# Two-layer model on one core: norm split between projection and scores, delta rule's gate behind the first naming, both key sides named together

## What is computed

```python
h2 = _rmsnorm(x, norm2[l])                    # x * rsqrt(mean(x*x) + EPS) * g
q = (xf @ w_pq).reshape(n_tok, P_HEADS, 2, P_DHALF)
s = jnp.einsum('thpd,phkd->thpk', q, sub_keys)
top_s, top_i = lax.top_k(s, P_TOPK)           # 16 of 128 keys on either side
cand_s = (top_s[:, :, 0, :, None] + top_s[:, :, 1, None, :]).reshape(...)
cand_i = (top_i[:, :, 0, :, None] * N_KEYS + top_i[:, :, 1, None, :]).reshape(...)
best_s, pos = lax.top_k(cand_s, P_TOPK)       # 16 of 256 pairs
idx = jnp.take_along_axis(cand_i, pos, axis=-1)
gate = jax.nn.softmax(best_s)
u = expert_u[it]
h = jax.nn.gelu(jnp.einsum('td,tkd->tk', xt, u), approximate=False)
v = expert_v[it]
y = jnp.einsum('tk,tkd->td', gt * h, v)       # 128 experts of every token
```

## Time and profile before

| | us |
|---|---|
| median of 3 runs | 1746.54 |
| lowest, highest | 1746.27, 1746.67 |
| span of the profiled execution | 1748.2 |
| TensorE, VectorE, ScalarE, GpSimd busy | 1545.4, 979.4, 440.9, 318.8 |
| gathers on GpSimd (L828), main and panels | 251.3 and 59.4 |

### The profile page before, as it was taken

One profiled execution on the slowest core, in us unless ns is written; L12 is line 12 of the kernel. 1 busy time (PEld: TensorE's weight loads), 2 busy tenths in 40 slices (PEclk: granted clock), 3 DMA queues, 4 the chain that ended last, 5 costly groups with the idle time before them and its releaser, 6 DMA issues.

```text
span 1748.2 us, 20696 instructions
## 1 busy us (share of the span) xinstructions
PE 1545.4 (88%) x8336; PEld 1016.7 (58%) x8336; DVE 979.4 (56%) x1882; ACT 440.9 (25%) x1004; POOL 318.8 (18%) x271
## 2 busy tenths in 40 slices
PE   8999999998988879878577676679999999999998
PEld 7867555557454534445233222249995486599953
DVE  3444443216877863579986656644755415356654
ACT  1143452103355631233243222221000024210001
POOL 0000000002135543343464454500000000000000
PEclk9999999999989989999789887899999999999999
DMA  5364222267999999999999999993453523354432
GB/s 226 145 223 163 98 97 97 109 247 319 425 385 406 424 419 389 421 422 415 422 420 421 422 422 421 422 382 145 151 188 145 201 94 127 130 196 163 175 144 96
DMA packets 55343, 468.32 MB, mean 268 GB/s; under 512 B 6736, under 2 KB 8144, under 8 KB 10704
## 3 DMA queue, kind: packets, MB, share of 16 engines
q0 software_dynamic: 36864, 268.45, 37.1%
q1 hardware_dynamic: 18384, 198.55, 29.9%
HBM read 465.93 MB, written 1.05 MB: 267 GB/s over the span
## 4 chain that ended last, share of the span: by engine, by line
PE 65%; DMA 17%; DVE 11%; issue 3%; ACT 2%; POOL 2%; SPq 0%; DVEq 0%; POOLq 0%; ACTq 0%
DMA main<-in_expert_uv,main 14%; PE ps L2401 14%; PE ps L2347 7%; PE ps L438 7%; PE ps L918 7%; PE ps L394 6%; PE ps L2558 6%; PE ps L2326 3%; DVE main L846 3%; PE ps L220 3%; DMA panels<-in_wall 2%; PE ps L2322 2%; PE ps L2633 2%; PE ps L434 2%; POOL main L828 1%
## 5 line engine op out<-in xcount | busy, mean ns | idle before, releaser
L918 PE MATMUL ps<-main 128*128 128x512 f32 x660 | 337.4, 660 | 120.8 <-ACT main L893 120.8
L828 POOL DMA_INDIRECT main<-in_expert_uv,main x208 | 251.3, 1208 | 381.9 <-PE ps L918 185.6
L846 DVE SCALAR_TENSOR_TENSOR main<-main 128x1024 f32<-128x1024 f32 x208 | 250.0, 1223 | 114.9 <-DMA main<-in_expert_uv,main 114.0
L918 PEld LDWEIGHTS ps<-main 128*128 128x128 f32 x660 | 132.6, 210 | 304.2 <-ACT main L893 161.0
L2347 PE MATMUL ps<-xT,panels 128*128 128x256 f32 x576 | 128.7, 386 | 1.8 <-DMA panels<-in_wall 1.8
L2347 PEld LDWEIGHTS ps<-xT,panels 128*128 128x128 f32 x576 | 111.1, 194 | 18.2 <-DMA panels<-in_wall 2.1
L881 ACT ACTIVATE main<-main 128x2 f32<-128x2 f32 x128 | 26.0, 203 | 365.6 <-DVE main L846 297.7
L394 PE MATMUL ps<-panels,xT 128*128 128x512 f32 x256 | 113.5, 597 | 0.0
L2401 PE MATMUL ps<-main 128*128 128x128 f32 x912 | 104.9, 275 | 0.0
L2401 PEld LDWEIGHTS ps<-main 128*128 128x128 f32 x912 | 103.4, 192 | 0.0
L918 PE MATMUL ps<-panels,main 128*128 128x512 f32 x152 | 76.3, 647 | 22.8 <-ACT main L893 22.8
(11 more groups left out here) (342 smaller groups left out, 2170.4 us busy)
## 6 DMA issues: line engine op xcount, KB each, us to landing
panels<-in_wall SPq DMA_DIRECT2D x85, 2048.0 KB, 8.1
main<-in_rows SPq DMA_DIRECT2D x14, 512.0 KB, 9.4
main<-in_expert_uv,main POOLq DMA_INDIRECT x208, 19.6
main<-in_sub_keys SPq DMA_DIRECT2D x2, 1024.0 KB, 12.8
panels<-in_wall SPq DMA_DIRECT2D x2, 1024.0 KB, 6.2
main<-in_wall SPq DMA_DIRECT2D x1, 2048.0 KB, 10.7
x<-in_x SPq DMA_DIRECT2D x2, 512.0 KB, 3.9
main<-in_pool_w SPq DMA_DIRECT2D x1, 1024.0 KB, 32.8
```

Source lines behind the costliest of these rows:

```text
L828: pool.indirect_dma_start(out=self.bufs[self.buf_of[r]], out_offset=None, in_=self.c.dram["expert_uv"], in_offset=bass.IndirectOffsetOnAxi ...
L846: dve.scalar_tensor_tensor(out=u, in0=u, scalar=1.0, in1=self.c.row(m, H2), op0=ALU.mult, op1=ALU.mult, accum_out=self.dots_at[:, m, q:q + ...
L918: mm = pe.matmul(self.c.ps[:, b, :], self.diags[self.of_pe(r) % DIAG_RING], v[:, half * HALF:(half + 1) * HALF], start=(q == 1), stop=(q = ...
```

## The change

Three things are changed. First, the norm: VectorE forms x times the norm row half by half as soon as each half of the output product is added; TensorE turns that and projects it, without the token's scale; ScalarE reads the turned halves ahead of squaring x, and puts the scale on when it reads the scores; VectorE scales the row in place to `h2` for the expert products. Second, delta1's gate stands behind `name0` in the order. Its output and squares move from scratch to tile 0's parts `Q_B` and `GATE_B`, which are buffer 7; buffer 7 is free from row 8 (`GATE_FREE`) and waits for the gate there, and row 0 waits for delta1's output product instead of its gate. Third, the naming handles both sides in one array: halves side by side, one comparison, one product and one sum over 32 numbers, with the first side's keys multiplied by 128 before.

```diff
-DELTA_FREE = 0
+GATE_FREE = 8
...
-        self.spans.update({7: [(0, end)], 8: [(DELTA_FREE, end)], 9: [(PARTS_FROM, end)], 10: [(PARTS_FROM, end)]})
-        self.spans.update({n: [(DELTA_FREE, SCRATCH_UNTIL)] for n in range(11, 14)})
+        self.spans.update({7: [(GATE_FREE, end)], 8: [(0, end)], 9: [(PARTS_FROM, end)], 10: [(PARTS_FROM, end)]})
+        self.spans.update({n: [(0, SCRATCH_UNTIL)] for n in range(11, 14)})
...
-                pool.wait_ge(*self.c.un.read_out("delta1.w"))
-            if r == DELTA_FREE:
+                pool.wait_ge(*self.c.un.full("delta1.o"))
+            if r == GATE_FREE:
...
+        if q == 0:
+            dve.wait_ge(*self.c.at("h2", m))
...
-        self.weighed, self.kb, self.wT, self.o = self.N_l, self.g_run, self.decay, self.X
+        self.weighed, self.kb, self.wT, self.o = self.N_l, self.g_run, self.decay, c.part(0, Q_B) if m else self.X
+        self.o_squared = c.part(0, GATE_B) if m else self.N
...
-    pe.wait_ge(*c.at("h2", m))
-    turn_tile(c, pe, t.h2)
+    for n in (0, 2):
+        pe.wait_ge(c.bank_read[n].sem, c.bank_uses[n])
+        c.bank_uses[n] += 1
+        pe.wait_ge(*c.at("x_weighed", m, n // 2 + 1))
+        for k in range(4):
+            mm = pe.transpose(c.ps[:, n, k * P:(k + 1) * P], t.h2[:, (2 * n + k) * P:(2 * n + k + 1) * P],
+                              c.mat("ident"))
+        mm.then_inc(c.turned.sem, 1)
...
+    read_turned_tile(c, act, t.h2T, 4 * m + 3)
     for b in (0, 2):
 
         act.wait_ge(c.bank_read[b].sem, c.uses_at[f"out.{m}"][b])
@@ -1658,7 +1668,6 @@
     if m:
         act.wait_ge(*c.at("x_mean", m))
         act.activation(t.stat[:, 2:3], t.stat[:, 1:2], ACT.Sqrt).then_inc(c.up("x_root"), 1)
-    read_turned_tile(c, act, t.h2T, 4 * m + 3)
...
-        act.activation(t.scores_of(g), un.view(x)[:, 0:2 * GROUPS[g][1], :], ACT.Copy).then_inc(un.freed(x), 1)
+        if g == 0:
+            act.wait_ge(*c.at("x_scale", m))
+        act.activation(t.scores_of(g), un.view(x)[:, 0:2 * GROUPS[g][1], :], ACT.Copy,
+                       scale=t.stat[:, 3:4]).then_inc(un.freed(x), 1)
...
-        at = c.x[:, m, q * HALF:(q + 1) * HALF]
-        dve.tensor_tensor(at, at, c.ps[:, bank, :], ALU.add).then_inc(c.bank_read[bank].sem, 1)
+        half = slice(q * HALF, (q + 1) * HALF)
+        dve.tensor_tensor(t.x[:, half], t.x[:, half], c.ps[:, bank, :], ALU.add).then_inc(c.bank_read[bank].sem, 1)
+        if q == 0:
+            dve.wait_ge(*c.norm_row_loaded.count(16 * (m + 1)))
+        dve.wait_ge(c.bank_read[bank].sem, c.uses_at[f"out.{m}"][bank])
+        dve.tensor_tensor(t.h2[:, half], t.x[:, half], t.norm_row[:, half], ALU.mult).then_inc(c.up("x_weighed"), 1)
     yield "out"
     dve.wait_ge(*c.at("x_squares", m))
     dve.tensor_scalar(t.stat[:, 1:2], t.stat[:, 0:1], 1.0 / D, EPS, ALU.mult, ALU.add).then_inc(c.up("x_mean"), 1)
-    dve.wait_ge(*c.at("x_root", m))
     if m:
-        step(dve.reciprocal(t.stat[:, 3:4], t.stat[:, 2:3]))
-    dve.wait_ge(*c.norm_row_loaded.count(16 * (m + 1)))
-    dve.scalar_tensor_tensor(out=t.h2, in0=t.x, scalar=t.stat[:, 3:4], in1=t.norm_row,
-                             op0=ALU.mult, op1=ALU.mult).then_inc(c.up("h2"), 1)
+        dve.wait_ge(*c.at("x_root"))
+        dve.reciprocal(t.stat[:, 3:4], t.stat[:, 2:3]).then_inc(c.up("x_scale"), 1)
+    dve.wait_ge(*c.at("x_scale", m))
+    dve.wait_ge(*c.turned.count(8 * m + 8))
+    dve.tensor_scalar(t.h2, t.h2, t.stat[:, 3:4], None, ALU.mult).then_inc(c.up("h2"), 1)
...
-        dve.tensor_scalar(halves[0], where, 4, None, ALU.logical_shift_right).then_inc(chain.next(), 1)
-        dve.tensor_scalar(halves[1], where, TOPK - 1, None, ALU.bitwise_and).then_inc(chain.next(), 1)
-        step(dve.tensor_copy(t.top_key[:, 0:2 * n], top_at.bitcast(U32)))
-        for x, half in zip(half_at, halves):
-            dve.tensor_copy(x, half).then_inc(chain.next(), 1)
+        dve.tensor_scalar(halves[:, :, 0], where, 4, None, ALU.logical_shift_right).then_inc(chain.next(), 1)
+        dve.tensor_scalar(halves[:, :, 1], where, TOPK - 1, None, ALU.bitwise_and).then_inc(chain.next(), 1)
+        dve.tensor_copy(t.top_key[:, 0:2 * n], top_at.bitcast(U32)).then_inc(chain.next(), 1)
+        dve.wait_ge(*chain.made(behind=1))
+        dve.tensor_copy(half_at, halves).then_inc(chain.next(), 1)
+        dve.wait_ge(*chain.made(behind=1))
+        side = keys_of[:, 0:n, 0, :]
+        dve.tensor_scalar(side, side, float(N_KEYS), None, ALU.mult).then_inc(chain.next(), 1)
+        dve.wait_ge(*chain.made(behind=1))
+        flat = half_at.rearrange("p k s -> p (k s)")
+        dve.tensor_tensor(hot, along(flat, TOPK), spread(t.iota, 2 * spots), ALU.is_equal).then_inc(chain.next(), 1)
         dve.wait_ge(*chain.made())
-        for side in range(2):
-            spot = half_at[side].unsqueeze(3).broadcast_to(shape)
-            lists = keys_of[:, 0:n, side, :].unsqueeze(2).broadcast_to(shape)
-            step(dve.tensor_tensor(hot, spot, t.iota.unsqueeze(1).unsqueeze(1).broadcast_to(shape),
-                                   ALU.is_equal))
-            step(dve.tensor_tensor(hot, hot, lists, ALU.mult))
-            step(dve.tensor_reduce(named[side], hot, AX_X, ALU.add))
-        step(dve.scalar_tensor_tensor(out=named[0], in0=named[0], scalar=float(N_KEYS), in1=named[1],
-                                      op0=ALU.mult, op1=ALU.add))
-        dve.tensor_copy(t.experts[:, TOPK * first:TOPK * (first + n)].bitcast(U32),
-                        named[0].rearrange("p h k -> p (h k)")).then_inc(c.up("experts_named"), 1)
+        by_spot = hot.rearrange("p (h k s) j -> p h k (s j)", h=n, s=2)
+        lists = t.top_key[:, 0:2 * n].rearrange("p (h s) j -> p h (s j)", s=2)
+        step(dve.tensor_tensor(by_spot, by_spot, lists.unsqueeze(2).broadcast_to([P, n, TOPK, 2 * TOPK]), ALU.mult))
+        step(dve.tensor_reduce(named, hot.rearrange("p (q s) j -> p q (s j)", s=2), AX_X, ALU.add))
+        dve.tensor_copy(t.experts[:, TOPK * first:TOPK * (first + n)].bitcast(U32), named)\
+           .then_inc(c.up("experts_named"), 1)
...
-    part("delta1", "S", "gate")
-    part("tile0", "pq0a", "scores0", "pq0b", "scores1", "top0", "best0", "name0", "pq1", "scores2", "top1", "best1", "name1", "pq2", "pq3", "scores3")
+    part("delta1", "S")
+    part("tile0", "pq0a", "scores0", "pq0b", "scores1", "top0", "best0", "name0")
+    part("delta1", "gate")
+    part("tile0", "pq1", "scores2", "top1", "best1", "name1", "pq2", "pq3", "scores3")
```

More of the change, by code:

```diff
@@ L162 @@
 ROW_STATS, GAIN, FIRST_STATS = 480, 472, 112
-ONCE = ("first_square", "first_variance", "first_scale", "scale_spread", "scales_kept", "minus_half", "bt", "zeros", "exp_a", "z_abs", "ln", "beta", "low_diff", "q_dec", "kb", "k_dec", "q_dec_b", "k_dec_b", "low", "lam_sums", "lam_exp")
+ONCE = ("first_square", "first_variance", "first_scale", "scale_spread", "scales_kept", "minus_half", "bt", "zeros", "exp_a", "z_abs", "ln", "beta", "low_diff", "q_dec", "kb", "k_dec", "q_dec_b", "k_dec_b", "low", "lam_sums", "lam_exp", "x_root")
 DOWN_PRODUCTS = 6
 PER_TILE = {"neg_top": 2, "N_l": LEVELS - 1, "both": 2 * LEVELS, "sum_read": 2, "a_kept": 2, "p": 2 * HEADS,
-            "best_less_max": 5, "gate_exp": 5, "experts_named": 5, "gates_made": 5, "down_product": DOWN_PRODUCTS}
+            "best_less_max": 5, "x_weighed": 2, "gate_exp": 5, "experts_named": 5, "gates_made": 5, "down_product": DOWN_PRODUCTS}
 class Signal:
@@ L1055, in delta_scalar @@
     act.wait_ge(*un.read_out(name("o")))
-    gated_norm_scalar(c, act, "delta", m, t.o, t.stat, t.N)
+    gated_norm_scalar(c, act, "delta", m, t.o, t.stat, t.o_squared)
     yield "gate"
@@ L1167, in delta_vector @@
     yield "S"
-    gated_norm_vector(c, dve, "delta", m, t.o, t.gate, 0, t.stat, t.N, floor=t.q_floor)
+    gated_norm_vector(c, dve, "delta", m, t.o, t.gate, 0, t.stat, t.o_squared, floor=t.q_floor)
     yield "gate"
@@ L1534, in __init__ @@
         self.left, self.cand = at(8, 4, N_KEYS), at(9, 2, TOPK * TOPK)
-        self.cand_left, self.hot = at(10, 2, TOPK * TOPK), at(8, 2, TOPK, TOPK)
+        self.cand_left, self.hot = at(10, 2, TOPK * TOPK), at(8, 4 * TOPK, TOPK)
         tops = base + 512 * 11
@@ L1538, in __init__ @@
         self.top_at, self.best_at = c.area(tops + 64, 4, TOPK), c.area(tops + 160, 2, TOPK)
-        self.half_at = [c.area(tops + 192 + 32 * n, 2, TOPK) for n in range(2)]
-        self.named = [c.area(tops + 256 + 32 * n, 2, TOPK) for n in range(2)]
+        self.half_at, self.halves = c.area(tops + 192, 2 * TOPK, 2), c.area(tops + 256, 2 * TOPK, 2)
+        self.named = c.area(tops + 384, 2 * TOPK)
         self.top_key = c.area(tops + 320, 4, TOPK)
@@ L1771, in tile_vector @@
             yield f"scores{CHOICE_SCORES[g]}"
-        shape = [P, n, TOPK, TOPK]
-        where, halves = t.best_at[:, 0:n].bitcast(U32), [x[:, 0:n].bitcast(U32) for x in t.named]
```

(6 more changed lines are left out.)

## The result

The changed kernel took 1758.89 us (median of 4 runs, 1755.22 to 1761.16) beside 1746.41 of the kernel before: a ratio of 1.0065, 95% interval 1.0052 to 1.0077. In a later comparison it was 1759.76 beside 1747.08, 1.0079 (1.0065 to 1.0093). The prediction was 1748.8 with a range up to 1751.8: sign right, size wrong by 10 us, outside its range.

The account below looks back on a forecast made before the run. The prediction took the expert-row gather's DMA to be the bound, its end tied to its restart at 499 to 500 us. Its terms, +5.15 - 1.7 - 1.1 = +2.3 us, gave 1748.8, range 1745.4 to 1751.8.

Parts of the forecast that it names:

- Start of the gather (2.5 us sooner): First gathered row issued at 411.9, not 414.34, by the moved gate and shorter naming; buys nothing by itself.
- 0.77 was forecast: The naming's saving ahead of row 0: 0.7 to 0.8 us per naming, bounds 0 and 1.1.
- Row 19 (+5.15): Row 19 waits for row 13's sum, not row 10's, as buffers are renumbered; DMA restarts 5.15 us later.
- TensorE reaches the sums 1.7 us sooner: Before the sums of rows 10 to 13: earlier panel, no idle gap, no clock drop; 1.7 us sooner.
- my lower bound of nothing: Low end of TensorE's gain before the sums: idle gap stays, clock drops, nothing gained; upper bound 3.3 us.
- I priced the panel at 11.9 us: Last query panel, issued at 414.24, now takes 11.9 us to land, not 9.1, arriving at 426.1.
- The dip (-1.1): DMA dip at 525 to 540 fills up, giving back 1.1 us: 0.6 by share, 1.7 by bytes.
- Tile 1 (0): VectorE's h2 about 1.7 us later, but it waits for landing rows anyway; between -0.5 and +0.5, taken as 0.
- Rival A: TensorE gains nothing before the sums, row 19 pays all 5.15: +4.05, 1750.6; chance 0.30, shared with another rival.
- the 69 to 69 in the prediction: At 427 to 431, panels and rows moved 69 packets each, so a panel gets two thirds of the bytes.

Follow-up runs that it names:

- 1: Changed kernel with the first rows' buffers dealt out in another order, so that row 19 waits for the sum of row 10 again: ratio 1.0036 to the kernel before.
- 2: Kernel before with only the first rows' buffer order changed, so that row 19 waits for the sum of row 13: ratio 1.0022.
- 3: Changed kernel with row 0 held until the last panel of the query projection is issued: ratio 1.0042 to the kernel before.
- 4: Changed kernel with row 0 held behind the last query panel and row 19 waiting for the sum of row 10 again: ratio 1.0007 to the kernel before.
- the eighth experiment: The kernel of 4 with tile 1's norm as in the kernel before, the split norm in tile 0 only: ratio 1.0020 to the kernel before.
- 9: Kernel before, unchanged, traced again: ratio 1.0001.
- 10: Changed kernel, unchanged, measured again beside the kernel before: ratio 1.0079.
- 13: Kernel before with panel buffers for rows from row 19 on instead of row 20, and nothing of the change: ratio 0.9997.
- 12: Kernel before with the naming of both sides at once and panel buffers for rows from row 19 on: ratio 1.0008.
- experiments 5 to 8: Kernel before with split norm, naming, or moved gate (row 19's wait as before) alone; then 4 with tile 1's old norm: 1.0007, 0.9994, 1.0004, 1.0020.

## Why the prediction missed

- **Start of the gather (2.5 us sooner): right.** 3.27 less the 0.73 of the whole program is 2.54. The naming takes 2.67 us for 3.60 (407.93 to 410.60 on VectorE), 0.93 less where 0.77 was forecast; the rest is the gate. It bought nothing by itself, as forecast.
- **Row 19 (+5.15): right,** within 0.1 us in experiments 1 and 2, counted from the start of the sums, and between 3 and 4 (502.44 and 497.28). The quotient written for it is not: 7.03 / 4 is 1.76. The 1.72 is the spacing of the starts: one row's four matmuls begin at 445.15, what follows them at 446.87.
- **TensorE reaches the sums 1.7 us sooner: wrong, the step that failed.** It was 3.2 us later. The panel landed at 426.79 where I had 426.1, but that is partly luck: it was issued 0.73 us sooner and took 13.3 us, not 11.9. The failure is behind it, where I took the product at full clock, to end at 433.4. By my own numbers TensorE ends the product ahead at 423.2 and then idles 2.9 us, and for a gap of 3.46 us in the earlier trace rows I had just charged 3.3 us of half clock. I moved the gap and put its price at nothing. The gap measured 4.36 us, the product ended at 436.7 (0.7 for the landing, 2.5 for the clock), so the panel after next was issued 3.3 us later than written, TensorE idled 2.61 us for it and fell to half clock a second time (8.83 for 7.03). 0.7 + 2.5 + 1.8 = 5.0, against the -1.7: 3.3. Experiments 3 and 4 take it away: the sums start 81 us behind the panel, as in the kernel before (82.6 and 81.3). No run shows the 1.7 us that I had forecast, and my lower bound of nothing (the clock drops, the gap stays) had no room for a second gap.
- **Whether the lead mattered at all.** I priced the panel at 11.9 us whatever the lead, from panels issued in the middle of the gather. That is about the right price on one side of a step, which lies between 0.1 behind and 0.8 ahead (12.4 us at 0.8 ahead, 12.9 to 13.9 at 2.4); the prediction never says that the naming alone would cross it.
- **The dip (-1.1): somewhat small.** The windows give 1.8 us back there (423 GB/s for 385), next to the 1.7 that the prediction had by bytes. Landings of single rows mislead: of 8.37 us at row 19, 5.34 were left at row 35 (548.91 and 554.25), but 7.9 again at row 86 (708.51 and 716.46).
- **Tile 1 (0): wrong by 1.3.** Row 86's product came 1.4 us late (1.7 forecast), and the DMA fell short at 740 to 760 (393 GB/s). I had argued that VectorE waits for rows there anyway; but row 92 is issued only when VectorE has used an earlier one. It leaves 28.2 us behind row 88 in all eight traces with tile 1's split norm and 26.8 in all eight without it, the eighth experiment's among them.
- **Behind the gather (not in the prediction): 1.4 us** (585.3 us from the last landing to the end, not 583.8; 1.7 in experiments 9 and 10). The last eight matmuls of the expert rows take 5.40 us, in part at half clock, and not 3.70, behind the same gap. Of the kernel before, and of the changed kernel:

```profile
1166.67 3.70 PE L918 MATMUL ps<-main 128*128 128x512 f32 x8 [2.80 <-ACT main L893]
```

```profile
1174.93 5.40 PE L920 MATMUL ps<-main 128*128 128x512 f32 x8 [2.79 <-ACT main L895]
```

It is 3.70 in the four traces that have no part of the change (before, again, 2, 13) and 5.3 to 6.7 in the other twelve. I have no cause for that: the naming alone should have nothing to do with it. It stays open.

Added up: 5.15 + 3.2 - 1.8 + 1.3 + 1.4 = 9.3 of the 9.6 us between the two spans.

Rival A came nearest, with the clock falling and 5.15 paid in full; but it kept the clock where it was and had it fall once.

## What to carry to other kernels

Two queues into the same DMA engines don't always share from the moment of issue. Where both began within 0.4 us of each other (12), they shared at once; otherwise the first had them for 3 to 5 us. Before making a gather start sooner, look whether a transfer that the critical engine waits for is issued within a few us of it; here it paid to be 0.1 us behind and cost 5 us to be 0.8 ahead. And when a forecast moves an idle gap of TensorE, move the half clock behind it too. When buffers are renumbered, list each row's predecessor: the 5.15 us could be read off before anything ran.

## What the hardware did that I had not expected

- The step itself: the panel's first packet moves 1.0 us behind its issue with row 0 0.1 us behind, 1.4 with row 0 0.8 us ahead (12), 3.5 with row 0 2.4 us ahead; and as the mirror of it row 0's first packets 4.5 us behind its issue (before, 414.34) or 1.9 (changed, 411.07, and 12). In the changed kernel each of the 16 DMA engines had moved some ten elements of the gather (161 / 16) between 414 and 417, before it came to the panel's first; after that they alternate. The Trainium skill (DMA: Bandwidth & Descriptors, Queues, rings and completion order) says that an engine drains a whole packet of about 9 to 17 descriptors from one queue before it goes to the next. The ten agree with that, and the even share behind them would too. The twelfth trace does not: there the gather had moved 15 elements, less than one per engine, when the panel's first moved. Nor is the 69 to 69 in the prediction a test of it, since those are counts of single elements. Why the panel waits in the one case and not in the other stays open.
- TensorE's clock behind nearly the same idle time: a gap of 3.79 us left the product behind it at 7.13 us (2), gaps of 3.66 and 3.73 gave 8.83 (3 and the kernel before again) and another of 3.73 gave 9.66 (13), one of 3.46 gave 10.20 (before). A shorter gap is not safer: behind 2.6 to 2.9 us the second product took 8.7 to 8.8 us in all five traces with 0.8 us of lead or more and without pauses. What follows the gap of 3.2 to 3.8 us spreads the sums' start by 3 us (79.6 to 82.6 in the table), and with it, I take it, the runs of one kernel.
- The pauses of TensorE in experiments 5 to 8, 2.2 to 2.6 us in each trace of that comparison and in none of any other. The chip alone is not the reason: experiments 1 to 4 ran on the same one without them. Their cause was not found.
